# Fourteen pairs of convolution tiles as seven block products, with gate tiles inside the attention units

## The reference, cut to what matters

```python
h = rms_norm(x, norm_g)
u = jnp.einsum('bsd,dc->bsc', h, w_in)                      # 68 tiles of 128 columns
v_c, b_c, c_c, z_c, q, k, v, z_a, gate_logits = jnp.split(u, SPLIT_POINTS, axis=-1)
y_c = b_c * causal_depthwise_conv(c_c * v_c, conv_w)        # 3 taps along the positions
y_a = jnp.einsum('bsc,cd->bsd', y_c * jax.nn.silu(z_c), w_conv_out)
...                                                         # q and k normed by head of 64
o = sliding_window_attention(q, k, v, sinks) * jax.nn.silu(z_a)   # 16 heads, window 128
y_b = jnp.einsum('bsc,cd->bsd', o, w_attn_out)
g_a, g_b = jnp.split(jax.nn.sigmoid(gate_logits + gate_b), 2, axis=-1)
return x + jnp.einsum('bsd,de->bse', g_a * y_a + g_b * y_b, w_out)
```

## Time and profile before

| | |
|---|---|
| median of 3 runs | 2413.71 us (2413.29 to 2416.06) |
| profiled execution: its span, first to last instruction | 2413.2 us |
| PE busy | 2391.0 us (99%) |
| DVE busy | 1458.8 us (60%) |
| ACT busy | 928.7 us (38%) |

### The profile page before, as it was taken

The page is one execution under the profiler, slowest core; times in us unless marked ns, Lnnn a source line. Parts: engine busy times, 40 slices in busy tenths (PEclk is TensorE's granted clock), DMA queues, the critical chain, the costliest instruction groups (busy, mean ns, idle before and its releaser), DMA issues.

```text
span 2413.2 us, 31544 instructions
## 1 busy us (share of the span) xinstructions
PE 2391.0 (99%) x11468; PEld 1990.5 (82%) x11468; DVE 1458.8 (60%) x2301; ACT 928.7 (38%) x1648; POOL 96.3 (4%) x114
## 2 busy tenths in 40 slices
PE   8999999999999999999999999999999999999998
PEld 6788888888888888888788888898888888888886
DVE  6747778777642243254654663374499888883335
ACT  6334454444531131142143243364355444442124
POOL 1000000000000000012000020012100000000000
PEclk9999999999999999999999999999999999999999
DMA  5111111111111131131111033263122222244323
GB/s 198 41 44 53 44 44 53 44 53 44 55 51 52 43 122 43 52 117 45 53 44 31 27 109 95 83 198 122 40 65 89 87 86 78 78 140 139 104 61 122
DMA packets 242954, 184.15 MB, mean 76 GB/s; under 512 B 6047, under 2 KB 224356, under 8 KB 241843
## 3 DMA queue, kind: packets, MB, share of 16 engines
q1 hardware_dynamic: 233920, 148.39, 20.2%
q0 software_dynamic: 5040, 18.78, 2.2%
q10 hardware_dynamic: 3906, 15.78, 2.0%
HBM read 150.42 MB, written 32.51 MB: 76 GB/s over the span
## 4 chain that ended last, share of the span: by engine, by line
PE 93%; DVE 4%; ACT 1%; DMA 1%; issue 1%; SPq 0%; ACTq 0%; DVEq 0%
PE bank L846 18%; PE bank L848 18%; PE bank L847 18%; PE bank L1383 4%; PE bank L1384 4%; PE bank L1385 4%; PE bank L1425 2%; PE bank L1424 2%; PE bank L1426 2%; PE bank L1194 1%; PE bank L1195 1%; PE bank L1196 1%; PE bank L1005 1%; PE bank L1477 1%; PE bank L1475 1%; PE bank L1476 1%
## 5 line engine op out<-in xcount | busy, mean ns | idle before, releaser
L846 PE MATMUL bank<-xhi,whi 128*128 128x512 f32 x1056 | 411.4, 390 | 0.5 <-DVE wlo L2282 0.5
L848 PE MATMUL bank<-xhi,wlo 128*128 128x512 f32 x1056 | 411.0, 389 | 0.0
L847 PE MATMUL bank<-xlo,whi 128*128 128x512 f32 x1056 | 411.0, 389 | 0.0
L2282 DVE TENSOR_TENSOR wlo<-wraw,whi 128x1024 fp32r<-128x1024 f32 (+1 forms) x202 | 238.8, 1182 | 151.7 <-ACT whi L1498 115.1
L1498 ACT ACTIVATE whi<-wraw 128x1024 fp32r<-128x1024 f32 (+1 forms) x131 | 130.9, 999 | 380.2 <-PE bank L848 176.8
L846 PEld LDWEIGHTS bank<-xhi,whi 128*128 128x128 f32 x1056 | 198.2, 188 | 42.3 <-DVE wlo L2282 0.7
L848 PEld LDWEIGHTS bank<-xhi,wlo 128*128 128x128 f32 x1056 | 198.2, 188 | 41.4
L847 PEld LDWEIGHTS bank<-xlo,whi 128*128 128x128 f32 x1056 | 198.2, 188 | 41.2
L1505 ACT ACTIVATE whi<-wraw 128x1024 fp32r<-128x1024 f32 x72 | 76.0, 1056 | 365.0 <-PE bank L848 361.2
L1671 ACT ACTIVATE Sx<-Sx,small 128x256 f32<-128x256 f32 x128 | 63.7, 499 | 224.0 <-DVE small L2482 224.0
L848 PE MATMUL bank<-ohi,wlo 128*128 128x512 f32 x256 | 99.6, 389 | 0.0
(11 more groups left out here) (470 smaller groups left out, 5392.8 us busy)
## 6 DMA issues: line engine op xcount, KB each, us to landing
wraw<-in_w_in_dram SPq DMA_DIRECT2D x85, 512.0 KB, 3.8
wraw<-in_ffn_w_up_dram SPq DMA_DIRECT2D x44, 512.0 KB, 3.8
ffn_spill<-ffn_value SPq DMA_DIRECT2D x22, 512.0 KB, 3.5
wraw<-in_xattn_wkv_dram SPq DMA_DIRECT2D x16, 512.0 KB, 4.1
wraw<-in_ffn_w_down_dram SPq DMA_DIRECT2D x16, 512.0 KB, 3.9
ffn_raw<-ffn_spill ACTq DMA_DIRECT2D x14, 512.0 KB, 4.5
wraw<-in_ffn_w_down_dram SPq DMA_DIRECT2D x16, 384.0 KB, 3.3
xraw<-in_x_dram SPq DMA_DIRECT2D x4, 1024.0 KB, 10.5
```

The source lines that it names most:

```text
L846: pe.matmul(acc, whi[slot][:, k, :], xh, start=(k == 0), stop=False)
L847: pe.matmul(acc, whi[slot][:, k, :], xl, start=False, stop=False)
L848: last = pe.matmul(acc, wlo[slot][:, k, :], xh, start=False, stop=(k == k_tiles - 1))
L2282: dve.tensor_tensor(wlo[slot][:, 0:n, :], wraw[slot][:, 0:n, :], whi[slot][:, 0:n, :].bitcast(F32), ALU.subtract).then_inc(s_wlo, 1)
```

## The change

The order of the first block's 72 tiles behind q, k and v is turned round. Ahead stand 24 filler tiles (`T_F`): gate b, z_a and gate a of each of 8 features in turn. 20 of them lie in the 32 attention units, 10 steps of 3 matmuls (30 matmuls) to a unit in place of 48, over three rotating banks; the other 4 follow behind. A finished tile goes to one of four buffers and by POOL to DRAM (`filler_spill`). The attention output goes to DRAM by blocks of positions (`store_o`, 16 transfers), and x comes back from its DRAM copy in three parts (`load_x_again`), the last behind the last block's output. Then follow 4 convolution tiles as dense ones, during which DVE and ACT make the activation forms out of x (`c_forms`), and 14 pairs (`conv_step`) in 7 products each. Gated attention output, convolution results and gates come back from DRAM; 8 tiles of w_attn_out and 8 of w_conv_out follow without gate tiles between them. The second block's code is the same but for the counts it waits on. The attention units are written out one by one in place of a loop over 8 blocks.

`HALVES_DONE` and `SPLITS_DUE` say where a filler's half is taken out and where the next weight is split: "early" ones stand ahead of `maxima` in DVE's stream (`halves_due(u, True)`), "late" ones behind it; a late split stands at the head of the next unit on ACT and DVE. Worked out for units 3 to 31 these tables give 15 early halves, 8 early splits and 10 late splits.

```diff
--- before.py
+++ after.py
+FILLERS = 24
+FILL_IN = 20
+FILL_STEPS = 2 * KT
+UNITS = 4 * NB
+UNIT_STEPS = tuple((FILL_IN * FILL_STEPS * (u + 1)) // UNITS - (FILL_IN * FILL_STEPS * u) // UNITS for u in range(UNITS))
+UNIT_END = tuple(accumulate(UNIT_STEPS))
+def unit_at(step):
+    u = next(u for u in range(UNITS) if UNIT_END[u] >= step)
+    return u, 2 * (step - UNIT_END[u] + UNIT_STEPS[u]) <= UNIT_STEPS[u]
+HALVES_DONE = [unit_at(KT * (m + 1)) for m in range(2 * FILL_IN)]
+SPLITS_DUE = [unit_at(FILL_STEPS * j) for j in range(1, FILL_IN)]
+T_X = T_F + FILLERS
+C_PLAIN = 2
+C_PAIRS = 2 * KT - C_PLAIN
...
+            def filler(first, end):
+                for step in range(first, end):
+                    m, k = step // KT, step % KT
+                    t, slot, h = T_F + m // 2, (T_F + m // 2) % 2, m % 2
+                    if k == 0:
+                        pe.wait_ge(s_wlo, t + 1)
+                        pe.wait_ge(s_free, 2 * T_F + m - 2)
+                    xh, xl = (x[:, k, h * HALF:(h + 1) * HALF] for x in (xhi, xlo))
+                    pe.matmul(ps(m % 3), whi[slot][:, k, :], xh, start=(k == 0), stop=False)
+                    pe.matmul(ps(m % 3), whi[slot][:, k, :], xl, start=False, stop=False)
+                    last = pe.matmul(ps(m % 3), wlo[slot][:, k, :], xh, start=False, stop=(k == KT - 1))
+                    if k == KT - 1:
+                        last.then_inc(s_acc, 1)
+            for u in range(UNITS):
                 if u == 2:
                     pe.wait_ge(s_qvar, 2)
                 if u >= 2:
                     turn(u - 2)
                 if u >= 3:
                     weigh(u - 3)
-                dense(u + T_CONV, u % 2, xhi, xlo, banks=CONV_BANKS)
+                filler(UNIT_END[u] - UNIT_STEPS[u], UNIT_END[u])
...
+            filler(FILL_IN * FILL_STEPS, (FILL_IN + 1) * FILL_STEPS)
+            turn(UNITS - 1)
+            weigh(UNITS - 2)
+            filler((FILL_IN + 1) * FILL_STEPS, (FILL_IN + 2) * FILL_STEPS)
+            weigh(UNITS - 1)
+            filler((FILL_IN + 2) * FILL_STEPS, FILLERS * FILL_STEPS)
+            pe.wait_ge(s_sf, UNITS)
+            pe.wait_ge(s_od, UNITS)
+            for n in range(2 * C_PLAIN):
+                t = T_X + n
+                dense(t, t % 2, xhi, xlo, free=(-2, -1) if n == 0 else (-2, -1) if n == 1 else None)
...
+            def conv_product(a, b, to, p, q, inc=1):
+                onto = (a, b) not in (("a11", "b11"), ("s1", "t1"))
+                pe.wait_ge(s_alo, 7 * p + (WEIGHT_ORDER.index(a) + 1))
+                o = ps(CBANKS[q][to])
+                if p == 0 and to == "x":
+                    pe.wait_ge(s_free, 2 * T_YB - 2)
+                if p == 1 and to == "x":
+                    pe.wait_ge(s_free, 2 * T_YB - 1)
+                if p == 0 and b in ct_at:
+                    pe.wait_ge(s_klo, FORM0 + 12)
+                for k in range(CHK):
+                    if p == 0 and b == "t4":
+                        pe.wait_ge(s_klo, FORM0 + 12 + k + 1)
+                    xh, xl = cform_of(b, k)
+                    pe.matmul(o, cahi[a][:, k, :], xh, start=(k == 0 and not onto), stop=False, skip_group_check=True)
+                    pe.matmul(o, cahi[a][:, k, :], xl, start=False, stop=False, skip_group_check=True)
+                    last = pe.matmul(o, calo[a][:, k, :], xh, start=False, stop=(k == CHK - 1), skip_group_check=True)
+                last.then_inc(s_m, inc)
...
+            def conv_step(p, q):
+                last = p == C_LAST
+                if not last:
+                    conv_product("s1", "t1", "z", p, q)
+                pe.wait_ge(s_cp, 3 * p + 1)
+                conv_product("s2", "t2", "y", p, q)
+                conv_product(*(("s1", "t1", "z") if last else ("a12", "b21", "x")), p, q)
+                pe.wait_ge(s_cp, 3 * p + 2)
+                conv_product("s3", "t3", "y", p, q)
+                if last:
+                    conv_product("a12", "b21", "x", p, q)
+                else:
+                    if p:
+                        pe.wait_ge(s_c, 4 * p - 2)
+                    conv_product("a11", "b11", "x", p + 1, 1 - q)
+                pe.wait_ge(s_cp, 3 * p + 3)
+                conv_product("a22", "t4", "y", p, q, 2 if last else 1)
+                pe.wait_ge(s_c, 4 * p + 1)
+                conv_product("s4", "b22", "z", p, q)
+            conv_product("a11", "b11", "x", 0, 0)
+            for p in range(C_PAIRS):
+                conv_step(p, p % 2)
...
+            def store_o(b):
+                pool.wait_ge(s_od, KV * (b + 1))
+                if b:
+                    pool.wait_ge(OS, 32 * b)
+                for g in range(2):
+                    pool.dma_start(o_parts[g, :, :, b * P:(b + 1) * P],
+                                   q32[64 * g:64 * g + 64, :, :, b * P:(b + 1) * P]
+                                   .rearrange("p i h s -> p (i h) s")).then_inc(OS, 16)
+            def load_x_again(n):
+                cols = (slice(0, HALF), slice(HALF, 7 * P), slice(7 * P, S))[n]
+                pool.wait_ge(OS, 32 * (4, 7, 8)[n])
+                pool.wait_ge(XR if n else s_spill, 16 * n if n else 16 * KT)
+                pool.dma_start(xr[:, :, cols], spill_v[:, :, cols]).then_inc(XR, 16)
+            for u in range(UNITS):
+                for m in range(1, 2 * FILL_IN, 2):
+                    if HALVES_DONE[m][0] == u:
+                        store_filler(m // 2)
+                if u % KV == 2 and u > KV:
+                    store_o(u // KV - 1)
+                if u == 5 * KV:
+                    load_x_again(0)
+            load_x_again(1)
+            store_filler(FILL_IN)
+            store_o(NB - 1)
+            load_x_again(2)
+            for j in range(FILL_IN + 1, FILLERS):
+                store_filler(j)
...
-                hold(dve, s_s, u + 1)
+                dve.wait_ge(s_s, u + 1)
...
+            def filler_out(m):
+                j, h = m // 2, m % 2
+                if j >= 4 and h == 0:
+                    dve.wait_ge(FILLED[j % 4], 16 * (j // 4))
+                evac(T_F + j, h, 0, fill[j % 4][:, h * HALF:(h + 1) * HALF], bank_at=m % 3).then_inc(s_free, 1)
+            def splits_due(u, early):
+                for j, (v, first) in enumerate(SPLITS_DUE):
+                    if first == early and v + (not early) == u:
+                        split(T_F + j + 2, (T_F + j) % 2)
+            def halves_due(u, early):
+                for m, due in enumerate(HALVES_DONE):
+                    if due == (u, early):
+                        filler_out(m)
+            dve.wait_ge(s_vt, 4)
+            for u in range(UNITS):
+                if u == 0:
+                    split(T_F + 1, (T_F + 1) % 2)
+                splits_due(u, False)
+                unit_lo(u)
+                if u >= 1:
+                    normalise(u - 1, (u - 1) % 2)
+                if u >= 2:
+                    turned_lo(u - 2)
+                if u >= 3:
+                    sum_o(u - 3)
+                if u == 1:
+                    query_var(1)
+                halves_due(u, True)
+                splits_due(u, True)
+                load_rq(u)
+                maxima(u)
+                halves_due(u, False)
+                if u == 1:
+                    query_inverse(1)
...
+            c_forms(0)
+            for h in range(2):
+                filler_out(2 * (FILLERS - 1) + h)
+            split(T_X + 1, (T_X + 1) % 2)
```

More of the change, by code:

```diff
@@ L2535, in attend @@
-            def attend(b):
-                for g in range(KV):
-                    u = 4 * b + g
-                    split(u + (T_CONV + 1), (g + 1) % 2)
-                    unit_lo(b, g)
-                    if not first_block(b) or g >= 1:
-                        normalise(u - 1, (g - 1) % 2)
-                    if not first_block(b) or g >= 2:
-                        turned_lo(u - 2)
-                    if not first_block(b) or g >= 3:
-                        sum_o(u - 3, b if g == 3 else b - 1, (g - 3) % 4)
-                    if first_block(b) and g == 1:
-                        query_var(1)
-                    load_rq(b, g, g % 2)
-                    maxima(b, g, g % 2)
-                    conv_part(b, g)
-                    if first_block(b) and g == 1:
-                        query_inverse(1)
@@ L2667, in _, with splits_due @@
-            branch(T_YB, 0, False)
-            branch(T_YA, 16, True)
+            def filler_out(m):
[3 more added lines that the diff above has]
+                evac(T_F + j, h, 0, fill[j % 4][:, h * HALF:(h + 1) * HALF], bank_at=m % 3).then_inc(s_free, 1)
+            def splits_due(u, early):
+                for j, (v, first) in enumerate(SPLITS_DUE):
+                    if first == early and v + (not early) == u:
+                        split(T_F + j + 2, (T_F + j) % 2)
@@ new lines, in _ @@
+            t = T_F + FILL_IN
+            splits_due(UNITS, False)
+            normalise(UNITS - 1, (UNITS - 1) % 2)
+            turned_lo(UNITS - 2)
```

(26 more changed lines are left out.)

999 lines of the change are left out of this document (641 added, 358 removed).

## The result

The changed kernel takes 2418.49 us (median of 20 runs, 2416.88 to 2420.19), the kernel before 2414.03 us (20 runs on the same chip, 2413.18 to 2416.90). The ratio is 1.0015 with a 95% interval of 1.0009 to 1.0022: 4.5 us slower, inside 0.2%. The forecast was 2412.4 us, 1.3 us faster, with a range of 2398 to 2428 and "within 0.2%" as the likeliest outcome. The time lies in the range, but the small step has the other sign.

The account below looks back on a forecast made before the run. PE's matmul stream was taken to bound the kernel, with a DVE-ACT chain hidden behind it. From 2413.2 us, - 38.1 (fewer matmuls) + 35.8 (attention waits) + 1.0 (entry) gave a span of 2411.9, median 2412.4; range 2398 to 2428.

Parts of the forecast that it names:

- The saving: In the 14 convolution pairs: 168 matmuls fewer, 38.1 us saved, a pair lasting 19.03 us.
- the cover taken from the FFN's steps: In the pairs: PE stays fed as in the FFN's steps, so the cost is nothing.
- The ring as the new bound: Attention: DVE-ACT chain `maxima`, `exps`, `unit_hi`, `unit_lo`, `normalise`, `turned_lo`, `sum_o`, `load_rq` sets the pace, costing 35.8 us more.
- The ring's size: Attention units 3 to 31: the DVE-ACT chain takes 311.2 us where PE needs 276.7, 10.73 us a unit.
- the bare unit: An attention unit without split or early evacuation: DVE-ACT chain of 9.77 us, rebuilt from unit 3, against PE's 9.54.
- rival B: Attention and its tail: some 40 POOL issues hold up DVE's scalings, at most 21 us, so 2434; chance 0.07.
- Entry into the products: Where the pairs' products begin, behind 4 dense tiles: PE waits 1.0 us, perhaps 3 us at the upper end.
- The tail: Behind the attention: x's last transfers take 11.9 us, hidden in 19 us, with a slack of 7 us.
- DRAM in place of SBUF: 24 tiles of 512 KB go out and back, each within 11 us of PE: hidden by matmuls.
- Rival A: Attention: the DVE-ACT chain gives way and units go at PE's 9.54 us, total 2376.6 us; chance 0.12.
- Rival C: Behind the attention: x, the forms or the last attention output come late, some 7 us, 2419.5 us; chance 0.12.

Follow-up runs that it names:

- e1: The changed kernel with the next unit's query high part ahead of `exps`, its low part behind `maxima`, late splits' low part behind `normalise`: 2380.68 us.
- e3: The changed kernel with 280 low-part matmuls of the fillers in the attention left out: 2416.79 us.
- e6: The changed kernel with the edits of e1 and e2 together: 2379.15 us.
- e2: The changed kernel with DVE's early half evacuations and early splits moved behind `maxima`: 2400.91 us.
- e4: The changed kernel with 22 in place of 20 filler tiles inside the attention: 2416.19 us.
- e7: e6 with unit 2's query square root behind `turned_hi(0)` on ACT, its inverse behind `turned_lo(0)` on DVE, late splits behind both: 2376.44 us.

## Why the prediction was right and where it was wrong

**The saving: right.** 168 matmuls are gone; pairs last (867.34 - 600.20) / 14 = 19.08 us against 19.03. The 0.05 us a pair are 0.7 us in all, nearly all of it at two places (619.3 and 856.3 us) where PE starts a step late. Else the cover taken from the FFN's steps held.

**The ring as the new bound: right**, shown by e1 to e3 and e6. Its reconstruction from unit 3 gave `maxima(2)` within 0.04 us, and the price of early work within 0.5 us (e2).

**The ring's size: the step that failed.** "The ring takes 29 x 9.77 + 27.9 = 311.2 us": it took 509.56 - 193.42 = 316.1 us between the `load_rq` of units 2 and 31, 10.90 us a unit in place of 10.73. Those 4.9 us turn "- 1.3" into plus 3.6. The counts of the tables (10 late splits, 15 early halves, 8 early splits) and their prices hold; what is off is the bare unit, in two places. The first is on ACT, from the small exponential of `exps` to `unit_hi`, here of unit 9 in the changed kernel:

```profile
263.43 0.19 ACT L1880 ACTIVATE small<-small 128x4 f32<-128x4 f32 x1
263.65 1.27 ACT L1871 ACTIVATE q_hi_twice<-q 64x512 fp32r<-64x512 f32 x2
```

and in the kernel before, ahead of the rows of unit 3 in the earlier trace rows:

```profile
207.20 0.19 ACT L1673 ACTIVATE small<-small 128x4 f32<-128x4 f32 x1
```

Of the 208.44 - 207.20 = 1.24 us there I took out the high part and the small instruction, 1.14, and so left 0.10, where 0.21 to 0.22 stand: 19 such units, 2.2 us. With a late split 1.16 to 1.17 stand where the sum has 0.10 + 0.98 = 1.08: 10 units, 0.85 us.

The second is on DVE, from `unit_lo` to `load_rq`. Unit 8, and then unit 9:

```profile
254.95 0.68 DVE L2797 TENSOR_TENSOR qlo<-q,q_hi_twice 64x512 fp32r<-64x512 f32 x1
...
257.01 1.22 DVE L2846 TENSOR_TENSOR ptlo<-bank,pthi 128x1024 fp32r<-128x1024 f32 x1
258.26 0.69 DVE L2808 TENSOR_TENSOR q<-bank,q 64x512 f32<-64x512 f32 x1
258.99 0.17 DVE L2832 COPY small<-rq 128x4 f32<-128x4 f32 x1
...
264.95 0.69 DVE L2797 TENSOR_TENSOR qlo<-q,q_hi_twice 64x512 fp32r<-64x512 f32 x1 [2.94 <-ACT q_hi_twice L1871]
...
267.14 1.22 DVE L2846 TENSOR_TENSOR ptlo<-bank,pthi 128x1024 fp32r<-128x1024 f32 x1
268.27 0.68 DVE L2808 TENSOR_TENSOR q<-bank,q 64x512 f32<-64x512 f32 x1
268.87 0.16 DVE L2832 COPY small<-rq 128x4 f32<-128x4 f32 x1
```

Unit 9 has 3.92 us, as unit 3 has in the earlier trace rows; unit 8 has 4.04. It goes by the number of the unit: odd ones have 3.92 and even ones 0.12 more, in the kernel before as well (its unit 4: 226.37 to 230.39, 4.02). The forecast read an odd one. The 14 even units among 4 to 31 are 1.6 us. What makes them longer is not shown. A third part, three copies that POOL held up (rival B below), is 0.5 us. 2.2 + 0.85 + 1.6 + 0.5 = 5.15, and 0.2 goes the other way in the rest.

**PE's loss against its wait rows.** The rows of `turn` and `scores` sum to 31.0 + 2.4 = 33.4 us, the loss by anchors is 41.9. In a unit that waits, the last matmul ahead of `turn` starts 1.88 us before it where 0.12 is PE's pace (245.20 to 247.08): 1.76 us, of which the row counts 1.60, because it begins at the end of that matmul's stay (0.28 us) and not where the next could have started. Counted from start to start against the same pairs of matmuls in e1, the starts of `turn` lose 35.9 us, those of `scores` 3.8 (most stops there are too short for a row), and the first matmuls behind a stop 2.1: 41.8 in all, which is the loss.

**Entry into the products: 1.0 us forecast, none measured**; the first product comes 4 x 10.88 = 43.52 us behind the start of the first dense tile at 556.68. **The tail: right**, hidden, and with more room than the 7 us I gave it: e4 took 21.8 us from it, and PE lost 9.6 + 1.5, so some 11 us were to spare. **DRAM in place of SBUF: nothing**, as forecast. That leaves 5.0 - 5.1 + 1.0 = 0.9 us between `turn(30)` and w_out that the sum does not have; 0.7 of them are in the pairs.

**Rival A** (the ring gives way by itself) did not happen; with the ring rearranged (e7) its time came out within 0.2 us. That closeness is in part luck: its sum holds the 1.0 us for the entry that did not come, and the kernel before was 1.4 us slower in e7's session than in the rows of the forecast. **Rival B** (POOL's issues hold the scalings up) did not happen in the changed kernel, but its mechanism is real. The 128 scalings in the changed kernel (ns min/median/max):

```profile
L2840 DVE TENSOR_SCALAR Sx<-Sx,small x128: 345/348/355, 179.6 to 515.4; 128x256 f32<-128x256 f32 x128
```

Of POOL's 36 issues up to 515 us none ran at the same time as a scaling, so these rows say nothing of what a meeting costs. Where they do meet, it costs: in e7 an issue of the attention output and the four scalings of a unit, and all its scalings,

```profile
232.52 1.42 POOL L859 DMA_DIRECT2D o_spill<-q  x2
...
233.16 1.43 DVE L2842 TENSOR_SCALAR Sx<-Sx,small 128x256 f32<-128x256 f32 x4
...
L2842 DVE TENSOR_SCALAR Sx<-Sx,small x128: 333/348/636, 177.9 to 472.3; 128x256 f32<-128x256 f32 x128
```

The four take 1.43 us in place of 1.14. In e7 five of the 128 take 0.61 to 0.64 us, in e6 five, in e1 one, each beside an issue of POOL; there PE does not wait for `turned_lo` in these units, and nothing is lost. In the changed kernel it is the copy of `load_rq` that meets them, in units 10, 18 and 26, and it is on the ring:

```profile
280.07 0.68 POOL L859 DMA_DIRECT2D o_spill<-q  x1 [7.36 <-DVE q L2808]
...
280.42 0.33 DVE L2832 COPY small<-rq 128x4 f32<-128x4 f32 x1
```

0.33 us in place of 0.16, three times: 0.5 us. (At four other units such a copy and an issue run at once and it takes its usual time; what decides is not shown.) The kernel before shows it too: the scaling of 387 ns in the earlier trace rows started at 607.13, beside the issue at 606.9 of the earlier trace rows. So the rule of the Trainium skill (SBUF — State Buffer, section "Who interferes with whom") that the forecast weighed, that such an instruction and GpSimd lock each other out, is borne out by these traces for the side of DVE, at 0.26 to 0.29 us a time for a scaling. The changed kernel escaped it by where its issues fall, which the forecast did not work out.

**Rival C** did not occur at 20 fillers; at 22 it did (e4).

## What to carry to other kernels

When the engine that bounds a stage gets less work, write out the chain of the others, instruction by instruction, before counting the saving: here two engines busy 70% and 53% of the attention formed a chain of 10.9 us against 9.54, and a reordering with not one instruction fewer gave 38 to 42 us back. Ask of each instruction in it whether it needs the one ahead; what only shares the queue belongs in the idle time of the other engine. And take such a chain from several units, even and odd ones: one unit told the bare length to 2%, but the slack of the kernel before wrong by a factor of nearly three.

## What the runs showed of the hardware

In e3 and e4 a PE that waited paid twice. In e3 the granted clock fell to 0.5 (1.2 GHz) twelve times in the attention, while PE waited on the ring; in e4 one wait of 9.6 us was followed by a half clock that lasted until past 560 us, when PE was in full work again. In the changed kernel itself, with waits of at most 1.6 us, the clock stayed at 1.00:

```profile
181.00:508.00 327.00, 293.98 (x1497) 244.68 (x1496) 230.28 (x656) 172.93 (x411) 21.01 (x34) 1.00 0.26 79
```

An issue of a transfer on POOL can hold DVE up: a scaling of 128x256 took 0.61 to 0.64 us beside one where 0.35 is its median (e6 and e7), and a copy of 128x4 took 0.33 us where 0.16 is (the changed kernel).
